# Gate and up products of both feed-forward stages by seven block products for eight

## What is computed

```python
def swiglu_half(x, g_pre, w_gate, w_up, w_down, g_post):
    h = rmsnorm(x, g_pre)
    y = (jax.nn.silu(h @ w_gate) * (h @ w_up)) @ w_down
    return x + 0.5 * rmsnorm(y, g_post)
```

## Time and profile before

| | us |
|---|---|
| median of 3 runs | 1528.04 (1527.54 to 1530.77) |
| span of the profiled execution | 1525.5 |
| PE busy | 1485.0 (97%) |
| DVE busy | 670.1 (44%) |
| ACT busy | 494.4 (32%) |
| POOL busy | 209.9 (14%) |

### The profile page before, as it was taken

One profiled execution on the slowest core, in us unless ns is written; L12 is line 12 of the kernel. 1 busy time (PEld: TensorE's weight loads), 2 busy tenths in 40 slices (PEclk: granted clock), 3 DMA queues, 4 the chain that ended last, 5 costly groups with the idle time before them and its releaser, 6 DMA issues. The chain is left out here.

```text
span 1525.5 us, 31235 instructions
## 1 busy us (share of the span) xinstructions
PE 1485.0 (97%) x12552; PEld 1367.5 (90%) x12552; DVE 670.1 (44%) x1021; ACT 494.4 (32%) x724; POOL 209.9 (14%) x199
## 2 busy tenths in 40 slices
PE   8999999999999999999998999989999999999996
PEld 7999999999888888877876887769989999999996
DVE  5333333222645765244476533456364434433224
ACT  6222223222521345221134333342353322323222
POOL 0111111000162000323200220021001111110000
PEclk9999999999999999999999999989999999999998
DMA  4222223222569978999997667837213222232221
GB/s 160 94 96 82 96 88 106 96 95 82 198 230 359 327 272 288 368 329 334 380 344 252 198 210 253 283 129 261 84 47 105 84 96 86 93 99 97 95 95 56
DMA packets 113366, 268.80 MB, mean 176 GB/s; under 512 B 15562, under 2 KB 18251, under 8 KB 112515
## 3 DMA queue, kind: packets, MB, share of 16 engines
q1 hardware_dynamic: 106610, 243.27, 46.5%
q0 software_dynamic: 6240, 23.28, 4.3%
q10 hardware_dynamic: 432, 1.05, 0.2%
HBM read 253.29 MB, written 14.26 MB: 175 GB/s over the span
## 5 line engine op out<-in xcount | busy, mean ns | idle before, releaser
L129 ACT ACTIVATE w_high<-w_raw 128x1024 fp32r<-128x1024 f32 (+1 forms) x179 | 199.6, 1116 | 705.6 <-PE psum L154 680.4
L133 DVE TENSOR_TENSOR w_low<-w_raw,w_high 128x1024 fp32r<-128x1024 f32 (+1 forms) x179 | 231.8, 1296 | 431.6 <-ACT w_high L129 430.2
L150 PE MATMUL psum<-h_high,w_high 128*128 128x260 f32 x1344 | 270.6, 282 | 0.6 <-DVE w_low L133 0.6
L154 PE MATMUL psum<-h_high,w_low 128*128 128x260 f32 x1344 | 270.9, 283 | 0.0
L152 PE MATMUL psum<-h_low,w_high 128*128 128x260 f32 x1344 | 270.4, 283 | 0.0
L150 PEld LDWEIGHTS psum<-h_high,w_high 128*128 128x128 f32 x1344 | 207.2, 188 | 1.5 <-DVE w_low L133 1.5
L154 PEld LDWEIGHTS psum<-h_high,w_low 128*128 128x128 f32 x1344 | 207.2, 188 | 0.0
L152 PEld LDWEIGHTS psum<-h_low,w_high 128*128 128x128 f32 x1344 | 206.6, 188 | 0.0
L493 POOL TENSOR_TENSOR silu<-silu,factor 128x520 f32<-128x520 f32 x44 | 79.1, 1798 | 505.3 <-ACT silu L514 505.3
L150 PE MATMUL psum<-mix_h_high,w_high 128*128 128x260 f32 x672 | 140.5, 290 | 1.2 <-issue 1.2
L152 PE MATMUL psum<-mix_h_low,w_high 128*128 128x260 f32 x672 | 136.4, 284 | 0.9 <-issue 0.9
(11 more groups left out here) (366 smaller groups left out, 2003.4 us busy)
## 6 DMA issues: line engine op xcount, KB each, us to landing
kv_ring<-in_cache_k SPq DMA_DIRECT2D x256, 256.0 KB
kv_ring<-in_cache_v SPq DMA_DIRECT2D x256, 256.0 KB
w_raw<-in_w_gu SPq DMA_DIRECT2D x86, 512.0 KB
w_raw<-in_w_dn SPq DMA_DIRECT2D x32, 704.0 KB
w_raw<-in_w_proj SPq DMA_DIRECT2D x44, 512.0 KB
spill<-h_f POOLq DMA_DIRECT2D x20, 260.0 KB
gates<-spill POOLq DMA_DIRECT2D x16, 260.0 KB, 4.2
w_raw<-in_w_merge SPq DMA_DIRECT2D x8, 512.0 KB
```

The lines of the kernel that those rows point to most:

```text
L129: act.activation(w_high[:, u, 0:nk, :], w_raw[:, u, 0:nk, :], ACT.Copy).then_inc(high_done, 1)
L133: dve.tensor_tensor(w_low[:, u, 0:nk, :], w_raw[:, u, 0:nk, :], w_high[:, u, 0:nk, :].bitcast(F32), ALU.subtract).then_inc(low_done, 1)
L150: pe.matmul(out[h], w_high[:, u, k, :], high[:, k0 + j, tok[h]], start=s, stop=False)
L154: mm = pe.matmul(out[h], w_low[:, u, k, :], high[:, k0 + j, tok[h]], start=False, stop=e)
```

## The change

Groups 0 and 1 stay as they were in their arithmetic. For groups 2 to 21 (G0 = 2) of each stage, the products are arranged as a 2 x 2 by 2 x 2 block product and done by Strassen's scheme in Winograd's form. The blocks of the weights are the even and odd chunks of the gate and of the up matrix; the blocks of the activations are the even and odd chunks at the first and the second half of the tokens. Seven products of 4 chunks and 3 passes each (12 matmuls) replace eight: 84 matmuls for 96.

Four sums of weights are formed for each group: S1 = up_even + up_odd and S2 = S1 - gate_even on DVE, S3 = gate_even - up_even and S4 = S2 - gate_odd on POOL (512 elements a partition each). Each is split in a high part on ACT and a low part on DVE, as are the whole gate block ("PA", 1024 elements, which gives the products P1 and P2) and the odd half of up ("P4"). The units of a group are PA, P5 (from S1), P6 (S2), P7 (S3), P4, and P3 (S4). Four sums of activations (t 0 to 3; 4 x 260 elements each) are formed once for each stage on POOL and split in the same way.

The results come together out of PSUM in halves of 260 columns: ACT copies P2, P5 and the sum P1+P6 to SBUF (p2, p5, u2), DVE forms g1 (gate, first half), c22 (up, second half), c12 (gate, second half) and the two hidden halves (hid1, hid2), POOL multiplies by the factor (g1 before and after its Silu, c22, and c12), and ACT takes two Silus. The order on ACT, DVE and POOL is written out, group by group; three tables (act_steps, dve_steps, pool_steps) count its steps, so that a wait can name one: `V(kind, n)` is a step of DVE, `A` of ACT, `G` of POOL, `at` a unit of PE. The split parts lie in a ring of slots. The raw weights have two places for whole groups (raws[n % 2]). All loops over groups are unrolled. `x` is used as working space, so in the second stage it is stored to DRAM first, and in both it is loaded again before the down products' end. The diff, cut:

```diff
+def unit_order():
+    order = [("gate", 1), ("up", 1)]
+    for n in range(G0, KF + 1):
+        for kind, m in (("PA", n), ("P7", n - 1), ("P5", n), ("P6", n), ("P4", n - 1), ("P3", n - 1)):
+            if G0 <= m < KF:
+                order.append((kind, m))
+    return order
...
+            at = (0, 8)
+        else:
+            c = 8 + 4 * ((r - 5 * NG7) % 4)
+            at = (c, c + 4)
+            r += 1
...
+BANK_A = {n: (n + 2) % 3 for n in range(G0, KF)}
+BANK_B = {n: 5 + n % 2 for n in range(G0, KF)}
+BANK_C = {n: 3 + n % 2 for n in range(G0, KF)}
...
+                    def load(n, m):
+                        sp.dma_start(raws[n % 2][:, m, :, :].rearrange("p k m -> p (k m)"),
+                                     w_gu[2 * n + m, :, :]).then_inc(gu_in[2 * (n % 2) + m], 16)
...
+                        load(n, 0)
+                        sp.wait_ge(gu_dve, V("P4", n - 2))
+                        load(n, 1)
+                    sp.wait_ge(gu_pool, G("S4", LAST - 1))
+                    sp.wait_ge(gu_dve, V("P4", LAST - 1))
+                    load_block(sp, w_dn, 0, nb, 0, NKD)
...
+                    def sum_three(n):
+                        pool.wait_ge(gu_in[2 * (n % 2)], arrived(n))
+                        pool.wait_ge(gu_in[2 * (n % 2) + 1], arrived(n))
+                        if n > G0:
+                            pool.wait_ge(gu_dve, V("P7", n - 1))
+                        pool.tensor_tensor(s34[:, 0, :, :], even(gate(n)), even(up(n)), ALU.subtract).then_inc(gu_pool, 1)
+                    def sum_four(n):
+                        pool.wait_ge(gu_dve, V("S2", n))
+                        if n > G0:
+                            pool.wait_ge(gu_dve, V("P3", n - 1))
+                        pool.tensor_tensor(s34[:, 1, :, :], s12[:, 1, :, :], odd(gate(n)), ALU.subtract).then_inc(gu_pool, 1)
...
+                    def gate_first(n):
+                        pool.wait_ge(gu_dve, V("g1", n))
+                        pool.tensor_tensor(g1[n % 2], g1[n % 2], fac1, ALU.mult).then_inc(gu_pool, 1)
+                    def gate_first_late(n):
+                        pool.wait_ge(gu_act, A("silu1", n))
+                        pool.tensor_tensor(g1[n % 2], g1[n % 2], fac1, ALU.mult).then_inc(gu_pool, 1)
...
+                    pool.wait_ge(gu_act, A("xw", KD - 1))
+                    pool.tensor_tensor(xe1, xe1, xe2, ALU.subtract).then_inc(gu_pool, 1)
+                    pool.wait_ge(gu_pool, G("t", 0))
+                    pool.tensor_tensor(t2[:, :, :], xo2, xe1, ALU.add).then_inc(gu_pool, 1)
+                    late(0)
+                    pool.wait_ge(norm_rec, norm_n + 1)
+                    sum_three(G0)
+                    pool.tensor_tensor(xe2, xo2, xe2, ALU.subtract).then_inc(gu_pool, 1)
+                    late(1)
+                    pool.wait_ge(gu_pool, G("t", 1))
+                    pool.tensor_tensor(xo1, xo1, t2[:, :, :], ALU.subtract).then_inc(gu_pool, 1)
+                    sum_four(G0)
+                    for n in range(G0, KF):
+                        if n >= G0 + 2:
+                            gate_second(n - 2)
+                        if n > G0:
+                            sum_three(n)
+                            sum_four(n)
+                        gate_first(n)
+                        if n > G0:
+                            up_second(n - 1)
+                        gate_first_late(n)
+                    gate_second(LAST - 1)
...
+                    def unit_high(kind, n):
+                        slot, free = SLOT[kind, n], FREE[kind, n]
...
+                            act.wait_ge(gu_in[2 * (n % 2) + 1], arrived(n))
+                            src, w = odd(up(n)), 4
+                        elif kind == "P5":
+                            act.wait_ge(gu_dve, V("S1", n))
+                            src, w = s12[:, 0, :, :], 4
+                        elif kind == "P6":
...
+                            src, w = s34[:, 0, :, :], 4
+                        else:
+                            act.wait_ge(gu_pool, G("S4", n))
...
+                    def gate_first_silu(n):
+                        act.wait_ge(gu_pool, G("g1f", n))
+                        act.activation(g1[n % 2], g1[n % 2], ACT.Silu).then_inc(gu_act, 1)
...
+                    sum_high(2, T3_HIGH, xe2)
+                    sum_high(3, t_hi[:, 8:12, :], xo1)
+                    if which == 1:
...
+                    for n in range(G0, KF):
+                        second_product(n)
+                        if n >= G0 + 2:
+                            gate_second_silu(n - 2)
+                        if n > G0:
+                            unit_high("P3", n - 1)
+                        if n < LAST:
+                            unit_high("PA", n + 1)
+                        unit_high("P7", n)
+                        gate_first_silu(n)
+                        fifth_product(n)
+                        second_sum(n)
+                        if n < LAST:
+                            unit_high("P5", n + 1)
+                        if n >= G0 + 2:
+                            hidden_high(n - 2)
...
+                    def sum_one(n):
+                        dve.wait_ge(gu_in[2 * (n % 2) + 1], arrived(n))
+                        if n > G0:
+                            dve.wait_ge(gu_dve, V("P5", n - 1))
+                            dve.wait_ge(gu_dve, V("S2", n - 1))
+                        dve.tensor_tensor(s12[:, 0, :, :], even(up(n)), odd(up(n)), ALU.add).then_inc(gu_dve, 1)
...
+                        dve.wait_ge(gu_in[2 * (n % 2)], arrived(n))
+                        dve.wait_ge(gu_dve, V("S1", n))
+                        if n > G0:
+                            dve.wait_ge(gu_dve, V("P6", n - 1))
+                            dve.wait_ge(gu_pool, G("S4", n - 1))
...
+                    gate_scale(1)
+                    sum_two(G0)
+                    unit_low("P6", G0)
+                    hidden(1)
+                    low(1)
+                    sum_low(2, T3_LOW, xe2, T3_HIGH)
+                    dve.wait_ge(gu_act, A("t", 3))
+                    dve.tensor_tensor(t_lo[:, 8:10, :], xo1[:, 0:2, :], t_hi[:, 8:10, :].bitcast(F32), ALU.subtract)
...
+                    for n in range(G0, KF):
+                        gate_first(n)
+                        if n >= G0 + 2:
+                            hidden_second(n - 2)
+                        if n < LAST:
+                            sum_one(n + 1)
+                        if n > G0:
+                            up_second(n - 1)
+                            unit_low("P3", n - 1)
+                        if n < LAST:
+                            unit_low("PA", n + 1)
+                        unit_low("P7", n)
+                        if n < LAST:
+                            unit_low("P5", n + 1)
+                        if n >= G0 + 2:
+                            hidden_low(n - 2)
+                        if n < LAST:
+                            sum_two(n + 1)
+                        if n > G0:
+                            hidden_first(n - 1)
+                        if n < LAST:
+                            unit_low("P6", n + 1)
+                        if n > G0:
+                            gate_second(n - 1)
+                        unit_low("P4", n)
...
+                                pe.wait_ge(gu_dve, V("hid1", n - 3))
+                            if n >= G0 + 2:
+                                pe.wait_ge(gu_act, A("p2", n - 2))
+                            else:
...
+                                mm = products("P2", BANK_B[n], slot + 2 * j + 1, j, j == 0)
+                        else:
+                            if kind == "P5":
...
+                    for kind, n in UNITS[2:]:
```

More of the change, by code:

```diff
@@ new lines, in dve_steps @@
+def dve_steps():
+    last = KF - 1
+    s = [("second", 0), ("second", 1), ("scale", 0), ("S1", G0), ("hid", 0), ("low", 0), ("PA", G0), ("t", 0), ("P5", G0), ("t", 1), ("scale", 1),
+         ("S2", G0), ("P6", G0), ("hid", 1), ("low", 1), ("t", 2), ("t", 3)]
+    for n in range(G0, KF):
+        s += [t for t in (("g1", n), ("hid2", n - 2), ("S1", n + 1), ("c22", n - 1), ("P3", n - 1), ("PA", n + 1), ("P7", n),
+                          ("P5", n + 1), ("low", n - 2), ("S2", n + 1), ("hid1", n - 1), ("P6", n + 1), ("c12", n - 1),
+                          ("P4", n)) if G0 <= t[1] < KF]
+    return s + [("c22", last), ("P3", last), ("hid2", last - 1), ("down", 0), ("low", last - 1), ("hid1", last),
+                ("c12", last), ("hid2", last), ("low", last)]
@@ L53, in ds @@
+ACT_AT = [{t: i + 1 for i, t in enumerate(s)} for s in ACT_STEPS]
+DVE_AT, POOL_AT = [{t: i + 1 for i, t in enumerate(s)} for s in (DVE_STEPS, POOL_STEPS)]
 def ds(i, n=1):
@@ new lines, in _, with silu, high @@
+                    second_high(1)
+                    factor_act(act, norm_n)
+                    if which == 0:
+                        for k in range(KD):
+                            scaled_act(act, xw, v_pre, k)
```

(6 more changed lines are left out.)

515 lines of the change are left out of this document (404 added, 111 removed).

## The result

The changed kernel takes 1680.53 us (1679.09 to 1685.86), the kernel before 1527.82 us (1527.54 to 1530.77) beside it: 1.1005 times as long, 95% interval 1.0985 to 1.1025. The forecast was 1638 with 1575 to 1688. The direction and the cause hold; the time is 42 us above the forecast, outside the 1620 to 1660 that the forecast gave as its own range and within the 1665 to 1685 of rival (d). The profiled execution has a span of 1677.3 us, 151.8 more than before, where the sum said 110.

A forecast was written before the change was run, and what follows sets the result against it. PE's matmul count bound the kernel before; afterwards load and detour waits would make periods 13.8 us, not 11.53. Stages of +59.5 and +50.9 gave +110 on a 1525.5 span, 1636, so a 1638 us median; range 1575 to 1688.

The forecast's parts named there:

- rival (d): Loops: POOL holds DVE back more than reckoned, or the load takes 3.6; period 14.5 to 15, 1665 to 1685 us; chance 0.11.
- PE's share: Loops: 84 matmuls of 119.5 ns need 10.04 us a group, 1.49 us less than before.
- Rival (b): Loops: PE stays the bound because load and detour overlap; period 10.04 us, about 1483 us in all; chance 0.11.
- DVE's sum: Loops: DVE's own work for a group adds up to 7.7 us, which fits within PE's 10.04.
- The loop through the load: Loops: the next group's load waits for P4's low part, and S1 waits for that load; 3.2 us.
- hid2 would be next at 2.2 us: Loops: with the load gone, the chain from P4's low part through g2's factor and Silu to hid2 limits, about 2.2 us.
- the detour: Loops: from P3's low part over POOL's S4 and g1 factor and ACT's steps to P5's low part; 4.8 us.
- The period: Loops: load, detour and DVE's steps between sum to 13.85 us a group, against 11.53 before.
- Start and tail: Stages: group 2's P4 low part ends at 58 and 1169.5 us; 3.8 us follow the last period.
- The reload of x: Down products: the reload lies under 16 blocks where PE is the bound and DMA 29% busy; costs nothing.
- The clock: Loops: PE's granted clock expected to hold at 1.00, with PE 72% busy in gaps of up to 2 us.
- rival (c): Loops: PE's clock falls to 1.2 GHz half the time and bounds those groups; 1700 us and more; chance 0.05.

The follow-up runs named there:

- e12: Changed kernel with two S4 places, S1 and x reload later, DVE doing POOL's loop work, and dependent DVE pairs separated by reordering: 0.9875 of before, 1501.3 us.
- e13: e12 with the start of both stages also moved from POOL to DVE, and the first stage's first Silu ahead of ACT's copies: 0.9807 of before, 1490.6 us.
- e1: Changed kernel without the weight loads of groups 4 to 21 in both stages: 1.0637 of before, 1616.9 us.
- e2: Changed kernel with a second place for S4, so POOL need not wait for P3's low part of the group before: 1.0541 of before, 1602.5 us.
- e5: Changed kernel with the reload of x moved behind six loads of down weights on SP's queue: 1.0929 of before, 1661.1 us.
- e11: Changed kernel with five small filler matmuls ahead of each group's P5 and P4 products: 1.0924 of before, 1670.7 us.
- e8: Changed kernel with two S4 places, S1 later, x reload later, and an earlier start of the groups: 1.0365 of before, 1583.3 us.

## Why the forecast was right in kind and 42 us short

**PE's share: right as a floor.** 84 matmuls a group need 10.04 us, and no run went below that: e12 and e13 have 10.20, and there DVE's instructions fill the period as closely as PE's. Rival (b), in which PE stays the bound, is nearly what the change does with its waits taken out: 0.9807 x 1527.8 is 1498 for e13, 15 above its 1483. The forecast's remark that DVE's sum is only 7.7 us holds as long as POOL does the rest.

**The loop through the load: right, 0.3 too small.** P4's low part ends at 191.25, S1 starts at 194.75: 3.50 us for 3.2. The forecast's remark that hid2 would be next at 2.2 us gave e1's 13.0 us within a tenth, but by luck: it starts POOL's factor for g2 0.5 us behind P4's low part, and the trace has it at 190.74, 0.5 us before that part's end. In return the factor took 1.13 us for 0.73 and hid2 1.05 for 0.43, both held by the exclusion that the forecast priced for the detour alone.

**The detour: right, 0.2 too small.** From the end of P3's low part (181.99) to P5's low part (186.97) lie 4.98 us for 4.8. S4 took 2.13 us for 1.29, and P7's low part was held to 1.77, as the rule that the forecast quoted has it. P5's low part stood idle 2.16 us for the forecast's "some 3", since P7's low part filled more of the detour. e2, which takes the detour away, shows that it was on the path.

**The period: 13.85 by the sum, 14.4 in the middle.** 3.50 + 4.98 and 1.44 for S2 to P6's low part in place of 1.37 make 14.4 with the other steps as put. Over the whole stage the mean is lower, since the first two distances of S1's starts are 11.5 and 13.8 us: (330.14 - 61.95)/19 = 14.12 us from the end of P4's low part of group 2 to that of group 21, and 14.12 in the second stage too: 0.32 x 38 = 12.2 us.

**Start and tail: mis-sized.** P4's low part of group 2 ends at 61.95 for 58 in the first stage, and at 1255.1 - 1198.8 = 56.3 us into the second for 49.7: POOL and DVE hold each other there too (low(0) took 2.62 us in the first stage and 2.71 in the second, for 0.70). The tail is 6.2 us for 3.8. Together 4.0 + 6.6 + 2 x 2.4 = 15.4 us.

**The reload of x: wrong.** I wrote that it lies under the down products and costs nothing, since PE is the bound there and DMA is busy 29%. I looked at the cover for the transfer, and not at what stands behind it on SP's queue: the next weight blocks. From the first down product on (264.66 and 1384.58 before, 336.35 and 1529.72 after) the first stage is 8.1 us longer and the second 6.7. e5 takes 6.3 and 5.0 of them away. So the reload's price is some 11 to 12.5 us: PE's holes behind it are 5.3 and 3.1 us, and the low clock behind each costs some 2 more. The rest is for the most part the low clock at the start of the down products, for which the forecast had no term: 0.58 in 1529.7 to 1533.7 us of after, with 21 matmuls for 35, which is 1.7 us; in e5 both stages have it.

Sum: 12.2 + 15.4 + 14.8 = 42.4 us, against 41.8 between the spans (the mixer was 0.8 shorter). So 1680 lies in rival (d)'s 1665 to 1685 in part by coincidence. Its mechanism, DVE held back by POOL more than reckoned, is seen in the period and in the start, but its period of 14.5 to 15 did not come, and 14.8 of the 42 us are the reload and the clock, which (d) does not have. The stated range holds the time only by the room that was left for (d).

**The clock: wrong in fact, small in time.** I expected 1.00 and wrote that under 0.95 rival (c) holds. In 60 to 320 us it was 0.92, but (c) as a price, 1700 and more, did not come: the waits for load and detour took the time whatever the clock was, as the steady 13.0 us of e1 at 0.94 and at 1.00 show. The Trainium skill, "TensorE: Matmul & The Clock Gate", section "HAM oscillation — how this bites in real kernels", tells of a kernel in which waits of 3 to 5 us between bursts of matmuls brought the clock down each time. Here it fell with waits of no more than 2.1 us, two in a period, against my reading of the first 30 us. No run shows a price of this fall in the loops. In the down products the low clock did cost time, since PE is the bound there: some 2.4 us behind the hole (20 matmuls fewer in 5 us), and some 3 us at their starts in e5. The mark was badly chosen: a lower clock shows that PE waits, not that it is the bound.

**Left open.** Why the loads of e11 landed in 3.2 us and not in 3.5, and with it whether the clock has any part in its 12 us, is not shown. e13's wait of 6.88 us at the start was not taken apart.

## What to carry to other kernels

Before work is taken from the bound engine, follow one group through the written order of the others: a buffer used once and a load issued behind the last step made a loop of 14.4 us out of engines whose sums were 10.0, 7.7 and 5.5. POOL was no spare engine beside a DVE that reads two operands from SBUF: handing 5.5 us of POOL's work back to DVE (2.5 us there) made the kernel nearly 3% faster. What is left then is DVE's own sum, 10.2 us, 0.16 above PE's. And ask of each transfer not only what hides it, but what waits behind it in its queue.

## What the runs showed of the hardware

- DVE and POOL excluded each other in both directions: P7's low part took 1.77 us for 0.69 beside S4, which itself took 2.13 for 1.29; in the start of e8 single instructions reached 3.39 and 3.41. A POOL fill that only writes took 0.97 us under a DVE instruction of that kind.
- The granted clock was 0.88 to 0.96 over stretches of 29 us with waits of PE of no more than 2.1 us each, PE 79 to 85% busy, and 1.00 in the run in which extra matmuls filled half of these waits; after 5.3 us without work it was 0.51 for 5 us.
- A 128-column fp32 matmul of ones gave two records and 0.22 us, so the 16 cost 3.5 us, as much as 29 of the kernel's own of 260 columns.
- A 2 MB load issued 0.7 us ahead of a block of 704 KB on SP's queue kept that block from being split until 10.1 us after its issue, with the DMA engines 93% busy in 346 to 351 us.
- Two DVE instructions of 260 elements start 0.34 us apart if independent and 0.45 if the second needs the first.
